# A two-layer hybrid decoder step: each FFN cut into three groups of hidden tiles, partial outputs parked in SBUF

## What is computed

```python
def _swiglu(x, wg, wu, wd):
    return (jax.nn.silu(x @ wg) * (x @ wu)) @ wd

def _layer(x, pe, w, cache):
    f1 = _swiglu(_rms(x, w['g_f1_pre']), w['w_f1_gate'], w['w_f1_up'], w['w_f1_down'])
    x = x + 0.5 * _rms(f1, w['g_f1_post'])
    ymix, st = _token_mixing(_rms(x, w['g_mix_pre']), w, cache)
    x = x + _rms(ymix, w['g_mix_post'])
    f2 = _swiglu(_rms(x, w['g_f2_pre']), w['w_f2_gate'], w['w_f2_up'], w['w_f2_down'])
    x = x + 0.5 * _rms(f2, w['g_f2_post'])
    gate = jax.nn.sigmoid(_rms(x, w['g_ple_pre']) @ w['w_ple_gate'])
    x = x + _rms(gate * (pe.astype(x.dtype) @ w['w_ple_proj']), w['g_ple_post'])
```

## Time and profile before

| | us |
|---|---|
| median of 3 runs (2469.26 to 2472.62) | 2471.02 |
| span of the profiled execution | 2469.1 |
| TensorE busy | 2372.0 |
| VectorE busy | 1173.3 |
| ScalarE busy | 825.8 |

### The profile page before, as it was taken

The page is one execution under the profiler, slowest core; times in us unless marked ns, Lnnn a source line. Parts: engine busy times, 40 slices in busy tenths (PEclk is TensorE's granted clock), DMA queues, the critical chain, the costliest instruction groups (busy, mean ns, idle before and its releaser), DMA issues.

```text
span 2469.1 us, 43109 instructions
## 1 busy us (share of the span) xinstructions
PE 2372.0 (96%) x18938; PEld 2282.6 (92%) x18938; DVE 1173.3 (48%) x1949; ACT 825.8 (33%) x1333; POOL 9.3 (0%) x18
## 2 busy tenths in 40 slices
PE   7999999999898999999999999999998999999997
PEld 6999999998578999999899999999985789999996
DVE  4333334775547333334663333356655573333346
ACT  4222223341445222323542222234315452222243
POOL 0000000000000000000000000000000000000000
PEclk9999999999899999999999999999898999999998
DMA  4222233221652222322222222223217422223221
GB/s 144 88 92 85 92 101 93 85 87 36 241 201 76 92 85 86 102 95 95 84 69 87 92 85 94 95 78 95 75 56 273 173 77 85 85 90 99 97 92 54
DMA packets 74467, 247.44 MB, mean 100 GB/s; under 512 B 14424, under 2 KB 16736, under 8 KB 74336
## 3 DMA queue, kind: packets, MB, share of 16 engines
q1 hardware_dynamic: 74336, 245.59, 29.7%
HBM read 238.68 MB, written 6.88 MB: 99 GB/s over the span
## 4 chain that ended last, share of the span: by engine, by line
PE 89%; DVE 5%; ACT 3%; DMA 1%; issue 1%; SPq 0%; DVEq 0%; ACTq 0%
PE psum L529 72%; PE psum L546 8%; PE psum L822 2%; DVE wl L1462 1%; DMA raw<-in_weights 1%; PE psum L885 1%; PE psum L919 1%; DVE x L1496 1%; ACT wh L1071 1%; PE psum L857 1%; PE psum L690 0%; PE psum L833 0%; PE psum L677 0%; PE psum L645 0%; PE psum L845 0%
## 5 line engine op out<-in xcount | busy, mean ns | idle before, releaser
L529 PE MATMUL psum<-xh,wh 128*128 128x272 f32 x3472 | 729.0, 291 | 12.4 <-DVE wl L1462 8.1
L1071 ACT CAST wh<-raw 128x1024 fp32r<-128x1024 f32 (+2 forms) x364 | 373.8, 1028 | 1092.3 <-PE psum L529 956.5
L529 PE MATMUL psum<-xh,wl 128*128 128x272 f32 x3472 | 723.2, 290 | 0.0
L529 PE MATMUL psum<-xl,wh 128*128 128x272 f32 x3472 | 720.5, 289 | 0.0
L1462 DVE TENSOR_TENSOR wl<-raw,wh 128x1024 fp32r<-128x1024 f32 (+2 forms) x364 | 436.0, 1198 | 291.8 <-ACT wh L1071 291.3
L529 PEld LDWEIGHTS psum<-xh,wh 128*128 128x128 f32 x3472 | 551.6, 190 | 17.1 <-DVE wl L1462 8.1
L529 PEld LDWEIGHTS psum<-xl,wh 128*128 128x128 f32 x3472 | 550.5, 190 | 0.0
L529 PEld LDWEIGHTS psum<-xh,wl 128*128 128x128 f32 x3472 | 546.7, 190 | 0.0
L529 PE MATMUL psum<-hh,wl 128*128 128x272 f32 x1232 | 255.0, 288 | 0.0
L529 PE MATMUL psum<-hh,wh 128*128 128x272 f32 x1232 | 254.7, 288 | 0.0
L529 PE MATMUL psum<-hl,wh 128*128 128x272 f32 x1232 | 254.0, 288 | 0.0
(11 more groups left out here) (261 smaller groups left out, 2178.7 us busy)
## 6 DMA issues: line engine op xcount, KB each, us to landing
raw<-in_weights SPq DMA_DIRECT2D x340, 512.0 KB, 3.5
kv<-in_kc SPq DMA_DIRECT2D x32, 672.0 KB, 8.0
kv<-in_vc SPq DMA_DIRECT2D x32, 672.0 KB, 6.7
raw<-in_weights SPq DMA_DIRECT2D x16, 320.0 KB, 4.8
raw<-in_weights SPq DMA_DIRECT2D x8, 384.0 KB, 4.9
x<-in_x SPq DMA_DIRECT2D x4, 544.0 KB, 7.2
out_x<-x SPq DMA_DIRECT2D x8, 272.0 KB, 2.1
out_v<-z SPq DMA_DIRECT2D x2, 816.0 KB, 4.3
```

Source lines behind the costliest of these rows:

```text
L529: ins = pe.matmul(T(t)[:, h, :], w, r[:, h, :], start=first and n == 0, stop=last and n == 2)
L1071: act.copy(wh[:, G % RING, 0:n], raw[:, G % 2, 0:n]).then_inc(hi.sem, 1)
```

## The change

**Order of the work.** The 22 hidden tiles of an FFN are cut into groups of 8, 7 and 7. TensorE makes the hidden tiles of a group, then all eight output tiles over that group's hidden tiles only, then goes to the next group. `hh` and `hl` hold eight tiles in place of 22, and the loop on TensorE is written out. The number and the shape of the matmuls stay as they were.

**Partial outputs.** Behind the first two groups, ScalarE copies each output tile from PSUM to `y_ff` (`down_part`). Before the second and the third group's output tiles, ScalarE writes the partial sum back into the PSUM tile (`seed`), and TensorE adds onto it (`onto`, no start flag). After the last group VectorE takes the tile out as before. An FFN has 16 such copies and 16 such seeds.

**Chunks.** A down chunk now is one output tile over one group: 8 or 7 blocks, and the 7-block ones are loaded and split at 128x896.

**End of an FFN.** The last three output tiles, in place of the last one, are made in two halves of the tokens (`TAIL` 3 for 1), and `y_mean_square` of half 0 stands behind the first of the three tiles of half 1.

**Layout.** `y_ff` no longer lies over `xl` but behind the shortened `hh` and `hl`. `raw` keeps two buffers in use.

The new file also has a second way to make an up tile, for tiles from number `PLAIN` on. `PLAIN` is 22, so no tile takes it, and its lines (`fast_pair`, `product`, `weight_sums`, `token_sums`, `h_fast`) are left out here. The only instruction of it that remains is a pair of 128x8 multiplies on VectorE at the start.

The groups, the tail and the layout:

```diff
+GROUPS = len(DOWN_BLOCKS)
+FIRST = (0, 8, 15, 22)
+
+
+PLAIN = 22
...
-TAIL = (1, 4, 1, 1)
+TAIL = (3, 4, 3, 1)
...
-        hh, a_h, _ = place("hh", [P, FT, 2, HALF], F32R)
-        hl, _, e_h = place("hl", [P, FT, 2, HALF], F32R)
...
+        hh, _, e = place("hh", [P, FIRST[1], 2, HALF], F32R, at=a_h)
+        hl, _, e = place("hl", [P, FIRST[1], 2, HALF], F32R, at=e)
...
+        y_ff, _, e_y = place("y_ff", [P, KT, 2, HALF], at=e)
...
+        def plain_at(f, g):
+
+            return 2 - 2 * ((FIRST[g + 1] - 1 - f) % 2)
```

TensorE:

```diff
-                n = s * FT
-                with pe.Fori(0, FT // 2 - 1) as f:
...
+            def up(L, s, g):
...
+                for f in range(max(FIRST[g], 2), FIRST[g + 1]):
...
+                    for j in range(2):
+                        G = L * X_ALL + up_at(s, f) + j
+                        freed = h_ready if j else gate_ready
+                        pe.wait_ge(freed.sem, freed.at(L, s * FT + f - 1))
+                        if f in FIRST:
+                            pe.wait_ge(yp_ready.sem, yp_ready.at(L, (2 * s + g) * KT))
+                        pe.wait_ge(lo.sem, G + 1)
                         for k in range(KT):
-                            ins = block3(j, G + j, k, xh[:, k], xl[:, k], k == 0, k == KT - 1)
+                            ins = block3(plain_at(f, g) + j, G, k, xh[:, k], xl[:, k], k == 0, k == KT - 1)
                         ins.then_inc(used.sem, 1)
...
+            def down(L, s, g):
...
+                def freed(d):
+                    if g:
+                        pe.wait_ge(seeded.sem, seeded.at(L, (2 * s + g - 1) * KT + d + 1))
+                    elif d >= 4:
+                        pe.wait_ge(yp_ready.sem, yp_ready.at(L, 2 * s * KT + d - 3))
...
+                for d in range(whole):
+                    freed(d)
+                    pe.wait_ge(lo.sem, c + d + 1)
+                    for k in range(blocks):
+                        if d == 0:
+                            pe.wait_ge(hl_ready.sem, hl_ready.at(L, s * FT + FIRST[g] + k + 1))
+                        ins = block3(d % 4, c + d, k, hh[:, k], hl[:, k], k == 0, k == blocks - 1, onto=g > 0)
+                    ins.then_inc(used.sem, 1)
...
                 for h in range(2):
...
+                    for d in range(whole, KT):
+                        if h == 0:
+                            freed(d)
+                            pe.wait_ge(lo.sem, c + d + 1)
+                        for k in range(blocks):
+                            ins = half_block(d % 4, c + d, k, hh[:, k], hl[:, k], h, k == 0, k == blocks - 1, onto=True)
+                        ins.then_inc((used if h else tail_done).sem, 1)
+                        if h and d == whole:
+                            y_mean_square(L, 2 * s, 0)
```

ScalarE (the last part is the end of a layer's first FFN; the second FFN's is alike):

```diff
+            def seed(L, s, g, d):
+
+                act.activation(T(d % 4), y_ff[:, d], ACT.Copy).then_inc(seeded.sem, 1)
...
+                        silu(L, s, f)
+                        split(G + 5)
+                        h_hi(L, s, f, g)
+                        if f < PLAIN - 1 and f < last:
+                            split(G + 6)
+                        continue
...
+                if last < PLAIN:
+                    for d in range(4 if g else 0):
+                        if d % 2:
+                            act.wait_ge(h_ready.sem, h_ready.at(L, t + d // 2))
+                        else:
+                            act.wait_ge(gate_ready.sem, gate_ready.at(L, t + d // 2))
+                        seed(L, s, g, d)
+                    return
...
+            def down_part(L, s, g):
+
+                for d in range(KT):
+                    G = L * X_ALL + down_at(s, g) + d
+                    act.wait_ge(used.sem, G + 1)
+                    act.activation(y_ff[:, d], T(d % 4), ACT.Copy).then_inc(yp_ready.sem, 1)
+                    if g and d < 4:
+                        act.wait_ge(yp_ready.sem, yp_ready.at(L, (2 * s + g) * KT + d + 1))
+                        seed(L, s, g, d + 4)
+                    split(G + RING)
...
+                for d in range(5, KT):
+                    half_square(L, 0, d, Y_FF, 0)
+                half_square(L, 0, 5, Y_FF, 1)
                 post_rstd(L, 0, 0)
-                split(c + 21 + RING)
+                split(c + 1)
                 enter(L, 1, L, 0, 0, [0])
-                split(c + 22 + RING)
-                enter(L, 1, L, 0, 0, range(1, 4))
-                half_square(L, 0, KT - 1, Y_FF, 1)
+                half_square(L, 0, 6, Y_FF, 1)
+                enter(L, 1, L, 0, 0, [1])
+                split(c + 2)
+                enter(L, 1, L, 0, 0, [2, 3])
+                half_square(L, 0, 7, Y_FF, 1)
                 enter(L, 1, L, 0, 0, [4, 5])
                 post_rstd(L, 0, 1)
                 enter(L, 1, L, 0, 0, [6, 7])
-                split(c + 23 + RING)
+                split(c + 3)
```

VectorE at the same end:

```diff
+                evac(L, 0, 5, 1)
                 join(L, 0, Y_FF, g, 0, [0], *to_mix)
-                weight_lo(c)
+                weight_lo(c + 1)
+                evac(L, 0, 6, 1)
+                add_square(L, 0, 5, 1)
                 join(L, 0, Y_FF, g, 0, [1], *to_mix)
-                weight_lo(c + 1)
+                weight_lo(c + 2)
                 join(L, 0, Y_FF, g, 0, [2, 3], *to_mix)
-                last_half(L, 0, Y_FF, G + X_D1, 1)
+                evac(L, 0, 7, 1)
+                add_square(L, 0, 6, 1)
                 join(L, 0, Y_FF, g, 0, range(4, KT), *to_mix)
-                weight_lo(c + 2)
+                weight_lo(c + 3)
```

More of the change, by code:

```diff
@@ L62, with ring_ff, up_at, down_at @@
 DOWN_BLOCKS = (8, 7, 7)
+GROUPS = len(DOWN_BLOCKS)
+FIRST = (0, 8, 15, 22)
+PLAIN = 22
+FAST = FT - PLAIN
+def ring_ff(s):
+    out = []
+    for g in range(GROUPS):
+        for f in range(FIRST[g], FIRST[g + 1]):
+            out += [("up", s, f, j) for j in range(2 if f < PLAIN else 4)]
+        out += [("down", s, g, d) for d in range(KT)]
+    return out
 C_OA = KT // 2
-X_F1, X_D1, X_IN, X_OB = CH_F1, CH_D1, CH_IN, CH_OUT
+C_FF = len(ring_ff(0))
+X_F1 = 0
+X_IN = X_F1 + C_FF
+X_OB = X_IN + C_IN
 X_OA = X_OB + KT
 X_F2 = X_OA + C_OA
-X_D2 = X_F2 + C_UP
-X_PJ = X_D2 + C_DOWN
+X_PJ = X_F2 + C_FF
 X_PG = X_PJ + C_PJ
 X_ALL = X_PG + C_PG
+RING_OF = (ring_ff(0) + [("in", 0, e, 0) for e in range(C_IN)] + [("ob", 0, d, 0) for d in range(KT)]
+           + [("oa", 0, d, 0) for d in range(C_OA)] + ring_ff(1) + [("pj", 0, d, 0) for d in range(C_PJ)]
+           + [("pg", 0, d, 0) for d in range(C_PG)])
+def up_at(s, f):
+    return RING_OF.index(("up", s, f, 0))
+def down_at(s, g):
+    return RING_OF.index(("down", s, g, 0))
+def is_fast(G):
+    what, _, f, _ = RING_OF[G % X_ALL]
+    return what == "up" and f >= PLAIN
+X_L1, X_L2 = down_at(0, GROUPS - 1), down_at(1, GROUPS - 1)
 A_BLOCKS = DB // P
@@ L89 @@
 RING = 4
+QW = 4 * P
+Q_SUM = (0, 1, 2, 3)
+Q_NAT = ((8, 9, 10, 11), (4, 5, 6, 7))
+UNITS = ((0, 0), (1, 1), (2, 3), (3, None))
 NCONST = K_RST + TOK
@@ L292, in width @@
             c = G % X_ALL
-            return (B_BLOCKS if X_OB <= c < X_OA else 2 * A_BLOCKS if X_OA <= c < X_F2 else KT) * P
+            what, _, g, j = RING_OF[c]
+            return (B_BLOCKS if what == "ob" else 2 * A_BLOCKS if what == "oa" else
+                    DOWN_BLOCKS[g] if what == "down" else KT) * P
+        loads = {}
+        held = [None] * 4
+        times = [0] * 4
+        pair = plain = 0
+        for G in range(DEPTH * X_ALL):
+            what, _, f, j = RING_OF[G % X_ALL]
+            if what == "up" and f >= PLAIN:
+                if j:
+                    continue
+                pair = 1 if f == PLAIN else 1 - pair
+                bufs = (2 * pair, 2 * pair + 1)
+            elif what == "down":
+                if j % 2 == 0:
+                    pair = 1 - pair if PLAIN < FT else 0
+                bufs = (2 * pair + j % 2,)
+            else:
+                bufs = (G % 2,)
+            loads[G] = []
+            for i, b in enumerate(bufs):
+                loads[G].append((b, times[b] + 1, held[b]))
+                times[b] += 1
+                held[b] = (G + 2 + i, G) if len(bufs) == 2 else (G + 1, None)
@@ new lines, in fast_count, with last_fast, raw_chunk, natural @@
+        def fast_count(G):
+            L, c = divmod(G, X_ALL)
+            _, s, f, _ = RING_OF[c]
+            return L * 2 * FAST + s * FAST + f - PLAIN
+        def last_fast(G):
+            G -= 1
+            while not is_fast(G):
+                G -= 1
+            return G - RING_OF[G % X_ALL][3]
+        def raw_chunk(b, n=8 * P):
+            q = (8, 10, 4, 6)[b]
+            return rq[:].rearrange("p q n -> p (q n)")[:, q * QW:q * QW + n]
+        def natural(G):
+            return Q_NAT[loads[G][0][0] // 2]
@@ L528, in block3 @@
                     for h in range(2):
-                        ins = pe.matmul(T(t)[:, h, :], w, r[:, h, :], start=first and n == 0,
-                                        stop=last and n == 2)
```

(22 more changed lines are left out.)

527 lines of the change are left out of this document (381 added, 146 removed).

## The result

| | before | after |
|---|---|---|
| median of 4 runs on one chip, us | 2470.76 (2469.26 to 2472.62) | 2518.30 (2517.94 to 2519.24) |
| span of the profiled execution, us | 2469.1 | 2516.2 |

The ratio is 1.0191, with a 95% interval of 1.0176 to 1.0205. 2519 us were predicted.

A forecast was written before the change was run, and what follows sets the result against it. TensorE, busy 96% of the span, bounds the kernel. Seams 20.6 and 7.8, ends 13.2, clock 6.1 sum to 47.7 us on 2469.1: 2516.8, as runs' median 2519 us; range 2503 to 2534, the forecast's own 2505 to 2533.

The forecast's parts named there:

- The signs: Profile after: right if 8 seed waits of about 2.4 us; wrong if "issue" gaps or over a third of waits with falls.
- What costs nothing: Inside the FFNs: same matmuls, written-out loop, ScalarE's copies, later seeds and split chunks, all hidden behind TensorE, adding no time.
- Seam from up to down: Groups two and three: TensorE waits for split, last `hh` and seed on ScalarE, 2.57 us, times 8 is 20.6 us.
- Seam from down to up: TensorE waits for ScalarE's last partial copy before the next group's up: 0.97 us with restart, times 8 is 7.8 us.
- The copy at 1176 us: Pattern in the trace before: TensorE waits for one ScalarE copy, 0.87 us, 0.97 with the restart.
- Ends: Four FFN ends: later mean square and joins, 3.4 us more twice and 3.2 twice, together 13.2 us; bounds nothing and 20.
- E: Start of the next stage's first matmul after an FFN, if nothing held it; times at the ends count from it.
- E+4.1, where TensorE asked for it at E+1.4: FFN end: VectorE has `xl` of block 1 ready at E+4.1, while TensorE asked for it at E+1.4.
- The clock: Falls to 1.2 GHz behind a third of 12 new waits (eight seams, four ends), 1.5 us each: 6.1 us; bounds 0 and 18.2.
- The rival with a fall at every new wait, short ones too: All 20 new waits lower the clock, 30 us in place of 6, so 2543 us; chance 0.10.
- The hidden-ends rival: The FFN ends cost nothing, as VectorE and ScalarE have idle time there: 2506 us; chance 0.10.
- The other side: Not slower: TensorE finds seeds and copies ready, seams cost nothing, waits at the ends come back: 2466 us; chance 0.04.

The follow-up runs named there:

- e3: Kernel after, with the gate chunk of groups two and three waiting for seven of the eight partial copies, the up chunk for the eighth: 2516.9 us.
- e1: Kernel before, with only TensorE's loop of ten rounds written out as straight code: 2472.8 us.
- e2: Kernel after, with the seeds of output tiles 0 and 1 moved on ScalarE ahead of the SiLU of the group's last hidden tile: 2497.4 us.
- e4: Kernel after, with the split of the next stage's third chunk moved earlier on ScalarE at each FFN end: 2513.1 us.
- e5: Kernel after, with the early seeds of e2 in group two alone, so only an FFN's first up-to-down seam is mended: 2505.7 us.
- e6: Kernel after, with the mean square of half 0 behind five blocks of the first half-1 output tile instead of all seven: 2522.3 us.
- e10: e6, with the taking-out and squaring of the first half-1 tile moved behind the 1/rms and first join: 2515.3 us.

## Why the prediction was right

- **The signs.** The eight seed waits came, of 2.1 us on average and 2.4 at most. Two signs that were set down as wrong came as well: gaps that the profile puts to "issue", which are the eighth copies by e3, and more than a third of the new waits with a fall behind them. An FFN's dense part grew by 8.2 to 9.8 us where 7 were forecast without falls, and had one or two falls more.
- **What costs nothing.** Right. No wait for a later seed, copy or chunk inside a down part is in the list, and e1 excludes the written-out code.
- **Seam from up to down.** 2.57 predicted, 2.27 measured, 18.2 for eight in place of 20.6. The order of the sum was right. The split takes 0.94 of the queue where 0.85 was set, but `hh` fills 0.55 until the seed starts, and the seed 0.54 until TensorE is released, where 0.65 was set for each. e2 confirms it as a whole.
- The Trainium skill, page "ScalarE: Activation LUTs", section "Step-by-step: what each stage is for", has ScalarE faster into PSUM than into SBUF. Here the seed is 620 ns and the `hh` copy of the same 544 columns 640, so the trace agrees in sign, and the gain is 0.16 us over the eight seams.
- **Seam from down to up.** 0.97 predicted, 0.89 measured, 7.1 in place of 7.8. The copy at 1176 us was the right pattern to read it from.
- **Ends.** From the last dense piece to the next stage's, with the six matmuls that the piece of after has more, the ends grew by 3.3, 4.5, 3.3 and 4.5, 15.5 in all, with a fall at each. Predicted were 13.2 without a fall. In the first FFN, where E is 428.19, the half-1 joins start at 441.31, E+13.1, for E+13.2. On the way two things were off. The step "E+4.1, where TensorE asked for it at E+1.4" overlooked that TensorE first asks for the third chunk's low part, at E+1.2: that is the 1.65 us wait. And the second mean square came at E+7.6 and not E+6.2, behind the fall. Neither moved the joins, since ScalarE's `post_rstd` (L1290) had its place in the queue at E+8.7 anyway, as its row shows: no idle time stands before it.

```profile
436.20 0.62 PE L703 MATMUL psum<-sq,con 128*128 128x272 f32 x2
...
436.41 0.41 ACT L1304 ACTIVATE sqx<-x 128x272 f32<-128x272 f32 x1
436.86 0.40 ACT L1290 ACTIVATE r<-psum 128x272 f32<-128x272 f32 x1
```

So at the first end the fall is hidden, and the 3.3 us are all order, for 3.4 predicted (the third end is alike: the 1/rms at 1682.78 has no idle time before it); at the second, 1.5 of the 4.5 are the fall (e4's comparison above), which leaves 2.9 for 3.2.
- **The clock.** The mis-sized term. A third of 12 waits was taken, 8 of 12 had a fall, and one FFN start more than before. With the two that were hidden left out, that is 7 x 1.54 = 10.8 us for 6.1. The rival with a fall at every new wait, short ones too, was wrong as well: none of the eight short seams had one.
- **Luck in the number.** What made the sum come out within 1 us is errors the other way: seams 3 us cheaper, and the other stages, predicted unchanged, 3 us shorter. These stages lost 37.3 us of clock in the trace after, and 44.5 to 51.0 in every other trace. The mechanism of the seams and ends does not rest on it, but the last few us do. The forecast's own range was also not what its bounds give: 2505 to 2533 were named, where no fall and 3 us less at the ends give 2510, and all 12 falls 2531.
- The Trainium skill, page "TensorE: Matmul & The Clock Gate", section "HAM oscillation — how this bites in real kernels", has one such loss for each burst of its example, where the waits are for DMA and longer (3 to 5 us). The traces, with waits of 2.1 us, agree in part: 20 of the 44 long seams (after, e3, e4, e5, e6, e10) had a fall behind them.

The hidden-ends rival (2506) fell with the ends' 15.5 us in the trace, and e4 shows that they move with the order of work. The other side (2466) needed seams of under 0.3 us, and they were 0.9 and 2.3. Open stays what decides, wait by wait, whether the clock falls, and so how much of a few us between two kernels is their own.

## What to carry to other kernels

Where one engine is dense, a new dependency costs the rest of its releaser's queue: read what stands ahead of the releasing instruction in its engine's order, and try to put it ahead of work that isn't waited for. Moving two seeds and lowering one count gave back 32 of 47.5 us, without touching a matmul. Before giving a small gain to a mechanism, look whether the granted clock fell in the same places in both traces: an edit that took out 7 us of waits showed as 1.4, and one worth 1.0 at its own place as 3.

## What was not expected of the hardware

The same wait of 2.1 us, in the same place of the same code, is followed by a stretch of lower granted clock in one trace and not in the next. In after it was so behind the first seam of all four FFNs and behind no second; in e4, with an edit only at the ends, behind two of the first seams; in e6 behind two first and two second; in e10 behind none:

```profile
253.28 42.34 PE psum L667 x336
```

That is e10's piece behind the first seam, 43.88 in after. A fall cost the 336 matmuls 1.54 us, and behind 0.76 us of idle time there was none in after's eight cases. The kernel before alone loses 47.9 us of clock, only two falls of it in the FFNs' dense parts. Outside the FFNs, where the change touches nothing, it lost 44.5 us and the kernel after 37.3: the difference of 7 us is more than most of the edits are worth.
